# Moving VectorE's selection rounds and the first loads of a two-layer hybrid decoder step

## The reference

```python
for l in range(DEPTH):                                   # 2
    mod = (c_act @ P['ada_w'][l] + P['ada_b'][l])        # scale, shift, gate
    x = x + 0.5 * mod[2] * swiglu(pre(x, 0), ...)
    (u_pool, hq, hf, hi, hg, aq, ak, av, iq, ik, iw, gl) = split(pre(x, 1) @ w_in)
    ya = pool_mix(u_pool)                                # windowed means
    yb = rmsnorm(hgrn_scan(hq, hf, hi)) * silu(hg)       # gated recurrence
    score = sum_h iw_h * relu(iq_h . ik) * IDX_SCALE     # the index
    top = top_k(score, 128)                              # keys of each query
    yc = attention(aq, ak, av, restricted to top)
    g = sigmoid(gl)
    merged = g0 * (ya @ w_ba) + g1 * (yb @ w_bb) + g2 * (yc @ w_bc)
    x = x + mod[5] * (merged @ w_out)
    x = x + 0.5 * mod[8] * swiglu(pre(x, 2), ...)
```

## Time and profile before

| what | value |
|---|---|
| median of 3 runs | 2799.78 us (2798.5 to 2801.74) |
| the profiled execution | 2792.26 us |
| its span, first to last instruction | 2790.4 us |
| TensorE busy with matmuls | 2684.0 us, 96% |
| VectorE, ScalarE, GpSimd busy | 33%, 30%, 39% |
| mean granted clock | 0.989 |

### The profile page before, as it was taken

How to read it: one execution, slowest core, us unless ns; L and a number is a source line. 1 busy time by engine, 2 the same in 40 slices (tenths; PEclk the granted TensorE clock), 3 DMA queues, 4 the chain that set the end, 5 groups by cost and what they waited for, 6 DMA issues and landing times. The chain is left out here.

```text
span 2790.4 us, 53847 instructions
## 1 busy us (share of the span) xinstructions
PE 2684.0 (96%) x22428; PEld 2543.9 (91%) x22428; DVE 925.9 (33%) x2319; ACT 826.5 (30%) x1310; POOL 1100.1 (39%) x886
## 2 busy tenths in 40 slices
PE   5999999999998999999999999999999999999998
PEld 3999998999887889999989999989988789899998
DVE  3111113266694441111131111134676834311111
ACT  2321222222454223212233212232234432332221
POOL 4444344233322354344454444542333124544443
PEclk9999999999999999999999999999999999999999
DMA  6334346212212243333233343341122124222322
GB/s 239 136 122 144 136 136 216 86 58 71 82 60 91 82 162 134 116 137 136 81 130 136 118 148 134 118 170 62 61 87 74 49 91 167 77 91 80 102 80 87
DMA packets 104038, 312.99 MB, mean 112 GB/s; under 512 B 18140, under 2 KB 42106, under 8 KB 86410
## 3 DMA queue, kind: packets, MB, share of 16 engines
q1 hardware_dynamic: 96194, 290.87, 30.4%
q10 hardware_dynamic: 7640, 19.17, 1.9%
HBM read 299.56 MB, written 10.66 MB: 111 GB/s over the span
## 5 line engine op out<-in xcount | busy, mean ns | idle before, releaser
L934 POOL TENSOR_TENSOR w_lo<-raw,w_hi 128x512 fp32r<-128x512 f32 (+1 forms) x800 | 1007.9, 1290 | 1647.1 <-ACT w_hi L991 1647.1
L2072 PE MATMUL bank<-h_hi,w_hi 128*128 128x260 f32 x3744 | 1068.2, 285 | 2.8 <-ACT silu_g L1038 2.4
L2073 PE MATMUL bank<-h_hi,w_lo 128*128 128x260 f32 x3744 | 1054.1, 282 | 0.0
L2074 PE MATMUL bank<-h_lo,w_hi 128*128 128x260 f32 x3744 | 1053.7, 281 | 0.0
L2072 PEld LDWEIGHTS bank<-h_hi,w_hi 128*128 128x128 f32 x3744 | 703.5, 188 | 42.1 <-issue 39.5
L2073 PEld LDWEIGHTS bank<-h_hi,w_lo 128*128 128x128 f32 x3744 | 703.8, 188 | 0.0
L2074 PEld LDWEIGHTS bank<-h_lo,w_hi 128*128 128x128 f32 x3744 | 703.6, 188 | 0.0
L991 ACT CAST w_hi<-raw 128x2048 fp32r<-128x2048 f32 (+3 forms) x220 | 378.3, 1720 | 481.4 <-PE bank L2074 377.3
L2072 PE MATMUL bank<-mid_hi,w_hi 128*128 128x260 f32 x1232 | 351.6, 285 | 0.0
L2074 PE MATMUL bank<-mid_lo,w_hi 128*128 128x260 f32 x1232 | 348.5, 283 | 0.0
L2073 PE MATMUL bank<-mid_hi,w_lo 128*128 128x260 f32 x1232 | 348.4, 283 | 0.0
(11 more groups left out here) (324 smaller groups left out, 3368.7 us busy)
## 6 DMA issues: line engine op xcount, KB each, us to landing
raw<-in_w SPq DMA_DIRECT2D x120, 1024.0 KB, 4.8
raw<-in_w SPq DMA_DIRECT2D x64, 512.0 KB, 4.1
ada_ring<-in_ada SPq DMA_DIRECT2D x78, 320.0 KB, 5.2
raw<-in_w SPq DMA_DIRECT2D x32, 768.0 KB, 4.2
ada_ring<-in_ada SPq DMA_DIRECT2D x82, 256.0 KB, 4.9
raw<-in_w SPq DMA_DIRECT2D x32, 640.0 KB, 4.0
ada_ring<-in_ada SPq DMA_DIRECT2D x78, 192.0 KB, 5.0
out_y<-x ACTq DMA_DIRECT2D x4, 1040.0 KB, 9.4
```

What stands on the lines that cost most here:

```text
L934: last = pool.tensor_tensor(w_lo[j][:, cols], raw[j][:, cols], w_hi[j][:, cols].bitcast(F32), ALU.subtract)
L2072: mm(out, wh(wb), xh(xb), start=(n == 0), stop=False)
L2073: mm(out, wl(wb), xh(xb), start=False, stop=False)
L2074: last = mm(out, wh(wb), xl(xb), start=False, stop=(n == len(blocks) - 1))
```

## The change

- **First loads.** The twelve constants are issued from ScalarE's queue. SyncE loads x first, then pieces 0 to 9, weight slot 0, pieces 10 to 15, weight slot 1. The statistics come after piece 9.
- **First norm.** Six tiles are multiplied by the root (`unit_tile`) before the second sums are taken, `scale_tile` is then a scale and shift from SBUF, and slot 1 of the weights is rounded in four pieces between ScalarE's tiles.
- **Recurrence.** The rotary steps 1 to 4 beside head 3 come after its levels.
- **Roots.** ScalarE gives the reciprocal root; `newton_rsqrt` has one instruction less. The one for `o_ms` comes after gate group (2, 0) and not after (2, 3).
- **Gates.** Tile 1's index is multiplied during the gates, in two pairs after gate groups (2, 2) and (2, 3) (`early_index`, `early_scores`); 8 of its 16 rounds run before the attention. `ybT` comes one gate group into slot 3 and three groups lie behind it.
- **Attention.** The rounds are at other steps (`ROUNDS_AT`): 4 in steps 0, 1, 6 and 11, 3 in steps 2 to 5 and 7 to 10. Tile 2's index is made before step 0. Fills move: 20 goes from step 11 to step 12, and so on, and fill 27 goes into the sample part. The reciprocal comes last in VectorE's step, behind mask, low values and fills.
- **Sample.** `q_blk` and `qi_blk` lie elsewhere and are filled in step 16.

```diff
-ADA_STAT = 12
+ADA_STAT = 10
...
 STEP_FILLS, _at = [], 4
-for _n in (1, 1, 1, 2, 2, 1, 2, 1, 1, 2, 1, 2, 1, 1, 1, 1, 2, 1):
+for _n in (1, 1, 1, 2, 1, 2, 1, 1, 2, 1, 2, 1, 1, 1, 2, 1, 1, 1):
     STEP_FILLS.append(range(_at, _at + _n))
     _at += _n
-SAMPLE_FILLS = ((28,), (29,), (30, 31), (32,), (33,), (34, 35), (36,), (37,), (38, 39))
-INDEX_AT = {0: (2, 0), 2: (2, 1), 4: (3, 0), 6: (3, 1)}
-INDEX_PAIRS = 2 * (TT - 1)
+SAMPLE_FILLS = ((27, 28), (29,), (30, 31), (32,), (33,), (34, 35), (36,), (37,), (38, 39))
+INDEX_AT = {4: (3, 0), 6: (3, 1)}
+INDEX_PAIRS = 2 * (TT - 2)
+EARLY_ROUNDS = 8
+ROUNDS_AT, MASK_AT = {}, {1: 1, 6: 2, 11: 3}
+for _t, _from, _steps in ((1, EARLY_ROUNDS, ((0, 4), (1, 4))), (2, 0, ((2, 3), (3, 3), (4, 3), (5, 3), (6, 4))),
+                          (3, 0, ((7, 3), (8, 3), (9, 3), (10, 3), (11, 4)))):
+    for _s, _n in _steps:
+        ROUNDS_AT[_s] = [(_t, _from + _i) for _i in range(_n)]
+        _from += _n
+    assert _from == TOP_PROMPT // 8
 TURNS = [min(s, 2 * 4) + 2 * max(0, s - 2 * 4) for s in range(STEPS + 1)]
 
...
-        keys += [(l, "rotT", t, part) for t in range(TT + 1) for part in (0, 1)]
+        for t in range(TT + 1):
+            keys += [(l, "rotT", t, part) for part in (0, 1)]
+            if t >= TT - 1:
+                keys += [(l, "early", 2 * (t - TT + 1) + i) for i in range(2)]
...
         probT = [area(f"probT{j}", [P, 2, TT, P], 84192 + 4096 * j) for j in range(2)]
         diag = [area(f"diag{j}", [P, P], 80096 + 512 * j) for j in range(4)]
+        score1 = area("score1", [P, 2 * P], 63712)
+        work1 = area("work1", [P, 2 * P], 64736)
...
+        q_blk = area("q_blk", [P, NB, NB, NKV, 4], 8320)
+        qi_blk = area("qi_blk", [HD, NB, NB, IDXH], 10368)
...
-            chain_.link(v.reciprocal(rt, rt))
             chain_.link(v.tensor_tensor(tmp, rt, rt, ALU.mult))
...
-            for n in range(2):
-                load_ada(n)
-            for name, tile in (("ada_b", ada_b), ("norm_g", norm_g), ("ident", ident), ("hgrn_lb", lb),
-                               ("pool_scale", pool_scale), ("col_select", col_select),
-                               ("spread_idx", spread_idx), ("spread_heads", spread_heads),
-                               ("gather_heads", gather_heads), ("page_table", page_ids),
-                               ("ada_select", ada_select)):
-                src = d[name]
-                if name == "spread_idx":
-                    src = src.rearrange("b (c h) -> b c h", h=IDXH)
-                sp.dma_start(tile[:], src).then_inc(const_loaded, 16)
-            sp.dma_start(onorm[:], d["hgrn_onorm"].partition_broadcast(P)).then_inc(const_loaded, 16)
-
             for k in range(2):
                 sp.dma_start(x[:, 4 * k:4 * k + 4, :], d["x"][:, 4 * k:4 * k + 4, :]).then_inc(x_loaded, 16)
-            for n in range(2, 12):
+            for n in range(10):
                 load_ada(n)
...
-            for j in range(2):
-                load_w(0, "up00", 0, j)
-                for n in range(12 + 2 * j, 14 + 2 * j):
-                    load_ada(n)
+            load_w(0, "up00", 0, 0)
+            for n in range(10, ADA_FIRST):
+                load_ada(n)
+            load_w(0, "up00", 0, 1)
...
-                        sp.wait_ge(side_full, SIDE[(l, "ybT", 2)] + 1)
+                        sp.wait_ge(logits_full, STEPS * l + 4)
...
+            for name, tile in (("hgrn_lb", lb), ("ada_select", ada_select), ("ada_b", ada_b), ("norm_g", norm_g),
+                               ("ident", ident), ("pool_scale", pool_scale), ("col_select", col_select),
+                               ("spread_idx", spread_idx), ("spread_heads", spread_heads),
+                               ("gather_heads", gather_heads), ("page_table", page_ids)):
+                src = d[name]
+                if name == "spread_idx":
+                    src = src.rearrange("b (c h) -> b c h", h=IDXH)
+                load_sp(tile[:], src).then_inc(const_loaded, 16)
+            load_sp(onorm[:], d["hgrn_onorm"].partition_broadcast(P)).then_inc(const_loaded, 16)
...
                 if sub == 0:
-                    for j in range(2):
-                        head(0, "up00", 0, j, None)
-                roots[0] += 1
+                    head(0, "up00", 0, 0, None)
...
+                    if sub == 0:
+                        s.copy(h_hi[:, k, 0:SEQ], scaled[:, k, :]).then_inc(h_hi_ready, 1)
...
+                    if sub == 0 and 1 <= k <= 4:
+                        act.wait_ge(w_loaded[1], slot_loads(0, "up00"))
+                        cols = slice((k - 1) * SPLIT_PIECE, k * SPLIT_PIECE)
+                        last = s.copy(w_hi[1][:, cols], raw[1][:, cols])
+                        if k == 4:
+                            last.then_inc(head_split[1], 1)
...
-                s.activation(sqrt_warm[:], ones[:, 0:1], ACT.Sqrt)
+                s.activation(sqrt_warm[:], ones[:, 0:1], ACT.Abs_reciprocal_sqrt)
                 act.wait_ge(ms_ready, 2 * l + 1)
-                s.activation(rot_ms[:, 1], rot_ms[:, 0], ACT.Sqrt).then_inc(root_ready, 1)
+                s.activation(rot_ms[:, 1], rot_ms[:, 0], ACT.Abs_reciprocal_sqrt).then_inc(root_ready, 1)
...
-                for t in range(1, TT + 1):
+                turned(l, 1)
+                gate_group(l, "ga0", 2, 0)
+                act.wait_ge(ms_ready, 2 * l + 2)
+                s.activation(o_ms[:, 1], o_ms[:, 0], ACT.Abs_reciprocal_sqrt).then_inc(root_ready, 1)
+                for t in range(2, TT + 1):
                     turned(l, t)
                     gate_group(l, "ga0", 2, t - 1)
-                act.wait_ge(ms_ready, 2 * l + 2)
-                s.activation(o_ms[:, 1], o_ms[:, 0], ACT.Sqrt).then_inc(root_ready, 1)
-                for group in range(4):
-                    gate_group(l, "ga0", 3, group)
+                    if t >= TT - 1:
+                        for i in range(2):
+                            src, _ = wait_side(act, l, "early", 2 * (t - TT + 1) + i)
+                            s.activation(src[:, 0:2 * P], src[:, 0:2 * P], ACT.Relu, scale=IDX_SCALE)\
+                             .then_inc(rel_ready, 1)
+                gate_group(l, "ga0", 3, 0)
...
+                for group in range(1, 4):
+                    gate_group(l, "ga0", 3, group)
...
-                relus(l, 1, 0)
+                relus(l, 2, 0)
                 fill(l, 0)
-                relus(l, 1, 1)
+                relus(l, 2, 1)
...
+                    if sub == 0:
+                        if k >= UNIT_TILES:
+                            unit_tile(k)
+                        v.tensor_scalar(scaled[:, k, :], scaled[:, k, :], md[:, 8 + k, 0:1], md[:, k, 0:1],
+                                        ALU.mult, ALU.add).then_inc(scaled_ready, 1)
+                        return
                     v.scalar_tensor_tensor(out=scaled[:, k, :], in0=x[:, k, 0:SEQ], scalar=md[:, 8 + k, 0:1],
...
+                    if sub == 0:
+                        v.tensor_tensor(h_lo[:, k, 0:SEQ], scaled[:, k, :], h_hi[:, k, 0:SEQ].bitcast(F32),
+                                        ALU.subtract).then_inc(h_lo_ready, 1)
+                        return
...
+            UNIT_TILES = 6
+
+            def unit_tile(k):
+
+                rstd, _ = wait_side(dve, 0, "norm", 0, 0)
+                link(v.tensor_tensor(scaled[:, k, :], x[:, k, 0:SEQ], rstd[:, 0:SEQ], ALU.mult))
...
-                        if hd > 0:
+                        if 0 < hd < HH - 1 or (hd == HH - 1 and n == 0):
                             rotary_step(l, BESIDE[hd - 1], n)
                     link(v.tensor_copy(decay[:, hd % 2], ends[-1][:]))
+                for step in (1, 2):
+                    rotary_step(l, BESIDE[HH - 2], step)
+                finish(HH - 1)
+                for step in (3, 4):
+                    rotary_step(l, BESIDE[HH - 2], step)
                 square_sums(l, "kv", 3, rot_sq[:, :, 0:2, :])
-                finish(HH - 1)
...
+                early_scores(l)
+                for n in range(EARLY_ROUNDS // 2):
+                    top_round(1, n)
...
+                for n in range(EARLY_ROUNDS // 2, EARLY_ROUNDS):
+                    top_round(1, n)
                 wait_side_taken(dve, l, "rotT", TT, 1)
                 v.tensor_copy(rotT_s[:], rotT[:, :, SEQ:COLS]).then_inc(rotT_copied, 1)
-                dve.wait_ge(causal_loaded, 16 * (l + 1))
                 make_mask(0)
-                scores_of(l, 1, 0)
+                scores_of(l, 2, 0)
                 fill(l, 0)
...
-                scores_of(l, 1, 1)
+                scores_of(l, 2, 1)
...
+            def early_scores(l):
+
+                dve.wait_ge(causal_loaded, 16 * (l + 1))
+                for h in range(IDXH):
+                    src, done = wait_side(dve, l, "early", h)
+                    dve.wait_ge(rel_ready, (2 * INDEX_PAIRS + IDXH) * l + h + 1)
```

(64 more changed lines are left out.)

33 lines of the change are left out of this document (16 added, 17 removed).

## The result

The changed kernel takes 2750.15 us in the median of 4 runs (2748.35 to 2751.49), beside 2800.76 for the kernel before, measured with it (4 runs, 2798.50 to 2802.08): ratio 0.982, 95% interval 0.980 to 0.984. The forecast was 2750.0.

The account below looks back on a forecast made before the run. TensorE, multiplying 2684.0 of 2790.4 us, bounds the kernel; only standstill and half clock can yield gains. Start 9.3 + waits 32.0 + modelled ends 2.7 + clock 10.1 - new waits 4.3 = 49.8, from 2799.8 to 2750.0; range 2736 to 2769.

Parts of the forecast that it names:

- The start: First loads and norm: last `ada_w` piece near 33, first weight product at 40.8; gain 9.3 us, bounds 5.5 and 11.7.
- The waits taken away: Mixers, both layers: TensorE's waits on `gate_f`, `yc_lo`, `qm`, `yab_lo`, `score` and at L2588 go or shrink, 32.0 us.
- modelled ends: Mixers: the list reads each wait some 0.15 us short; over 18 waits, 2.7 us more gain.
- ACT_TABLE_LOAD: Last `rotT` transposes: table load takes 1.28 us without the 1.38 drain; chain ends at 728.4, TensorE waits 0.7 per layer.
- Does VectorE hold the pace: Attention steps 8 to 11: with 13 rounds, not 16, VectorE needs 23.5 us against TensorE's 25.2, margin 1.7.
- L2588: TensorE's wait for `qi_blk`, 4.2 us in 2, goes: VectorE fills it in step 16, fill 27 covers ScalarE's page copies.
- The clock: Mixers: four low-clock stretches within 6 us of removed waits go; gain 10.1 us, bounds 0 and 10.1.
- the clock's rival: Mixers: low clock stays, since a wait is not enough to cause it; 10.1 not gained, 2760 us; chance 0.17.
- The start gives only the issue time: First loads: only the constants' issue time, 5.5 us, is gained; 2754 us; chance 0.07.
- VectorE becomes the bound: Attention step 11 ends late, each layer keeps the 5.60 us wait: 2761, or 2768 with low stretches; chance 0.14.
- nothing: Waits move to the next join and first loads end at GpSimd's squares: no gain, 2800 us; chance 0.02.
- The slower one: Last transposes' bank wait costs the chain's lateness beyond 729.7; from 27 us it eats the gain, at 30: 2805; chance 0.03.

Follow-up runs that it names:

- the late root's: The changed kernel with ScalarE's root for `o_ms` two gate groups later, behind gate group (2, 2) and the first two relus: 2765.86 us.
- the start alone: The kernel before with only the change's first loads, statistics and first norm: 2786.44 us, ratio 0.9964.
- the second profile of before: The kernel before, unchanged, profiled once more with 12 runs of its own: 2796.88 us, profiled span 2795.0.

## Why the prediction was right, and where it was lucky

- **What bounds it**: right. 34.6 us of the profiled difference are time that TensorE no longer stands still.
- **The start**: forecast 9.3, measured 7.2 between the two profiles and 8.1 by the means. The step that failed is the count of what the queue moves before the last piece, "11.6 MB": it was 12.73, and the 1.1 MB more are 2.9 us at 390 GB/s, by which the piece came later than 33. The stream itself began near 3 us, as forecast: 4 us after the start it had moved little (13 and then 192 GB/s in two windows of 2 us), and 12.73 MB at 395 GB/s from 3 us on end near 35.2. The dip between 11 and 15 us makes most of the rest; in it the constants' queue has a share of the engines' time beyond its bytes (packets, MB, share of 16 engines, in the view of the DMA queues of after):

```profile
q1 hardware_dynamic: 620, 1.11, 78.1%
q10 hardware_dynamic: 444, 0.08, 16.5%
```

  That share alone does not explain the dip, because from 13.0 to 13.5 us the engines are busy for 0.57 of the time only; how the constants cause it stays open. The new delay, unit tiles behind the last piece, was 1.5 us in after as forecast (piece ends at 36.50, the last of five unit tiles before `ada_rows` at 37.96), and smaller in some of the other profiles: in the late root's, VectorE's five tiles end at 36.78 and the piece at 36.67. The upper bound of 11.7 has no working; the 1.5 us hidden would have given 10.8. By the Trainium skill, "DMA: Bandwidth & Descriptors", section "Issuing engines are not separate DMA queues", issuing on a second engine saves only the time that the issuing takes. By that rule the gain would have been 5.5 here, and the two traces come near it: of the 5.8 us by which the last piece is multiplied earlier (41.69 and 35.88), the bytes give 0.6, since only 12.95 - 12.73 = 0.22 MB left the path and not the slot's 1.05, and some 5.2 are the time in which the engines had stood empty. No run separates the two, so this is my working from the two DMA views.
- **The waits taken away**: forecast 32.0, less 4.3 for new ones, 27.7 of listed waits, and 2.7 for modelled ends on top. Measured: idle time fell by 34.6, of which the start alone made 6.2, so 28.4, in the same measure as the 27.7. Each named wait went. The new ones are 1.5 at L2402 (forecast 1.4), 1.0 behind `gate_e` and 0.6 at L2469, together 3.1 where 4.3 was forecast. The 2.7 is not borne out: what a modelled end hides counts as busy time, and busy time less the clock's cost fell by 0.6 in all, within the 4.4 by which it differs between profiles anyway.
- **ACT_TABLE_LOAD**: VectorE's chain ended at 721.33. The forecast's 728.4 is in the time of before's trace; at the first four groups of `rotT` transposes the changed kernel is 7.4 ahead, so it stood for 721.0. The wait behind it was 0.7 in each layer, as forecast; it ended with the first early score, which waited for the product and ScalarE and not for the chain. By the Trainium skill, "ScalarE: Activation LUTs", section "What ACT_TABLE_LOAD costs", a drain of 1.38 us would be added. The changed kernel's trace differs from it: the load stands right behind the copy before (713.59) and the root right behind the load:

```profile
713.61 1.28 ACT L1289 ACT_TABLE_LOAD   x1
714.90 0.22 ACT L1289 ACTIVATE o_ms<-o_ms 128x20 f32<-128x20 f32 x1
```

- **Does VectorE hold the pace**: it does, by 3.8 us in four steps and not 1.7. The failed step is TensorE's 25.2, which I took from the start of VectorE's stretch to the point where TensorE stood; a whole set of four steps is 28.7 to 29.1 of TensorE's work. With the right figure the spread of the rounds would have been costed at nothing once fill 20 is moved, as it measured. The prediction named the mechanism of the two large waits, 11.2 us (fill 20 behind four rounds), and gave fill 20's place and the reciprocal's as the cure. Fill 20's place is the cure; the reciprocal's is worth the small `gate_f` waits alone, 1.7 when it was put back.
- **L2588**: the wait was of the right size, but the prediction gave both halves of the edit as its cause, and either is enough.
- **The clock**: forecast 10.1. By the two first profiles it is 5.5, by the second profile of before 8.6. The four stretches named went. What was not foreseen is that others grow: 6.8 and 6.8 us at the head of the gates, with no wait in front. Part of that is the chance of one execution, since the other profiles have 3.4 to 10.2 there. The sign "at most one per mixer" did not come out in layer one, which has the stretches at 464.1 and 675.8.
- **The total**: 9.3 + 27.7 + 2.7 + 10.1 = 49.8 against a profiled 40.7, so the sum was 9 too high against its own execution. Its terms are too large by 2.1 for the start, 3.1 for the modelled ends (nothing is left for them) and 4.6 for the clock, and 0.7 too small for the listed waits. That it hit the median to 0.2 us is luck: that execution of before lay 7.5 below its median, and the forecast took the same 49.8 off the median. By the granted clock of the runs the slower executions of before spend more time at the low level, so the change had more to take away there; that the two errors cancel was not foreseen.
- **The rivals**: the clock's rival is half true, and its remark that a wait is not enough holds too: behind L2588's wait of 2.1 us a low stretch came in two of the six cases in the three profiles that have it. "The start gives only the issue time" fell in its price, though most of the gain is that time. "VectorE becomes the bound" and "nothing" fell; built, the former measured 2765.2 and not the 2768 with low stretches, for which the prediction took their whole lengths and not the time that TensorE is busy in them (2766). The slower one has its mechanism, and its slope of one to one, behind 1.4 us of slack, was measured over the first 7 us; its decision point was not tried, and by its own rule that would be about 25.6 us (half of 49.8, and the 0.7), not 27.

Not settled: what brings the low stretches at the gates' head and in the sample part, where no wait stands ahead, and why their number differs between executions of one kernel. The waits on `yab_lo` and `score`, 7.4 in all, went with the new place of `ybT` and of tile 2's index, which were not undone by themselves.

## What to carry to other kernels

Before a selection loop is thinned out, ask what stands behind it: the same rounds in the same step cost nothing once no matmul's bank was queued behind the last of them. Undo the halves of an edit one at a time and together, since here one of two edits carried 11.6 us and the other none by itself, but both together 15.1, and at another place either one was enough. Count what is issued behind the last needed load as well, because its packets may run beside it. And take an account that separates standing still from the low clock before comparing two profiles: here the clock differed by 3 us between two executions of one kernel, as much as some of the edits are worth.

## What the runs showed of the hardware that was not expected

- Between executions of one kernel the time at the low clock changes: it is 54.6 and 61.4 us in the two profiles of before, and the granted clock is 0.983 to 0.991 in 33 runs of it on one chip, which spread over 17.5 us.
- The same stretch of idle time is cheaper or dearer by where the low clock falls: behind the wait, matmuls run at half speed (7.1 us of waits cost 11.6); over the wait, part of it costs nothing (15.2 us of waits where there were 1.5 cost 15.7, with TensorE busy in 6.07 of 10.2 us at the low level).
- Small packets weigh more than their bytes: between 11 and 15 us the 444 packets of the constants took 16.5% of the engines' time for 0.08 MB, beside 78.1% for the 1.11 MB of the weights in 620.
- A load that is issued behind another on the same queue can move most of its bytes before the first has landed: some 0.85 of the 1.05 MB of the weight slot issued at 26.82 us had moved when the last piece, issued at 26.27, landed at 35.84.
